# Weight units in a ring of six slots whose low part is written over the loaded data, in place of four raw slots and four split pairs

## The reference

```python
xn = rmsnorm(h, attn_norm[l])
proj = xn @ w_in[l]
y_mla = mla_branch(proj, q_norm[l], w_uq[l], kv_norm[l], w_ukv[l], cos, sin) @ w_mla_branch[l]
y_fox = fox_branch(proj, fox_f_bias[l]) @ w_fox_branch[l]
gates = jax.nn.sigmoid(proj[..., OFF_G:])
g_mla, g_fox = gates[..., :D_MODEL], gates[..., D_MODEL:]
h = h + (g_mla * y_mla + g_fox * y_fox) @ w_out[l]
hn = rmsnorm(h, mlp_norm[l])
u = jnp.square(jax.nn.relu(hn @ w_up[l]))
h = h + u @ w_down[l]
...
return rmsnorm(h, final_norm)
```

## Time and profile before

| | us |
|---|---|
| median of 3 runs | 1279.23 |
| lowest, highest | 1279.23, 1279.76 |
| profiled execution | 1279.13 |
| its span, first to last instruction | 1277.3 |
| TensorE matmuls busy | 1268.6 (99%) |
| weight loads of TensorE busy | 1053.9 (83%) |
| VectorE busy | 761.6 (60%) |
| ScalarE busy | 596.9 (47%) |
| GpSimd busy | 137.8 (11%) |

### The profile page before, as it was taken

How to read it: one execution, slowest core, us unless ns; L and a number is a source line. 1 busy time by engine, 2 the same in 40 slices (tenths; PEclk the granted TensorE clock), 3 DMA queues, 4 the chain that set the end, 5 groups by cost and what they waited for, 6 DMA issues and landing times.

```text
span 1277.3 us, 14314 instructions
## 1 busy us (share of the span) xinstructions
PE 1268.6 (99%) x5666; PEld 1053.9 (83%) x5666; DVE 761.6 (60%) x759; ACT 596.9 (47%) x688; POOL 137.8 (11%) x239
## 2 busy tenths in 40 slices
PE   9999999999999999999999999999999999999997
PEld 7888888888888888888888888888888888888886
DVE  6676566646766577566665655454455656554543
ACT  6654345444555444444454444333344444453443
POOL 0122001103221111110111110000000101100000
PEclk9999999999999999999999999999999999999999
DMA  8799856756887688787778786666667787856663
GB/s 329 250 295 277 260 176 214 230 188 200 272 266 213 203 297 276 233 249 228 253 229 259 224 260 194 195 196 195 189 222 235 235 246 237 285 168 215 195 197 116
DMA packets 82851, 293.88 MB, mean 230 GB/s; under 512 B 11288, under 2 KB 11872, under 8 KB 82144
## 3 DMA queue, kind: packets, MB, share of 16 engines
q1 hardware_dynamic: 67248, 243.04, 58.9%
q0 software_dynamic: 14528, 48.00, 13.1%
q10 hardware_dynamic: 1008, 1.92, 0.4%
HBM read 269.45 MB, written 23.47 MB: 229 GB/s over the span
## 4 chain that ended last, share of the span: by engine, by line
PE 99%; DVE 0%; ACT 0%; DVEq 0%; POOL 0%; issue 0%; ACTq 0%; POOLq 0%
PE bank L593 97%; PE bank L694 1%; PE bank L676 0%; PE bank L674 0%; PE bank L718 0%; PE bank L697 0%; PE bank L679 0%; PE bank L677 0%; DVE resid L1317 0%; DVE final L1326 0%; ACT square L983 0%; DVEq L335 0%; POOL kr_low L478 0%; ACT std_col L987 0%; DVE rstd_col L1323 0%
## 5 line engine op out<-in xcount | busy, mean ns | idle before, releaser
L1029 DVE TENSOR_TENSOR hl<-raw,hl 128x1024 fp32r<-128x1024 f32 x451 | 550.4, 1230 | 465.1 <-ACT hl L813 464.7
L813 ACT ACTIVATE hl<-raw 128x1024 fp32r<-128x1024 f32 x451 | 475.7, 1059 | 600.0 <-PE bank L593 570.5
L593 PE MATMUL bank<-hl,hn_hl 128*128 128x512 f32 x1536 | 348.5, 389 | 0.0
L593 PE MATMUL bank<-hl,u_hl 128*128 128x512 f32 x1536 | 348.5, 389 | 0.0
L593 PE MATMUL bank<-hl,x_hl 128*128 128x512 f32 (+1 forms) x1536 | 344.9, 385 | 0.0
L593 PEld LDWEIGHTS bank<-hl,hn_hl 128*128 128x128 f32 x1536 | 288.3, 188 | 59.9
L593 PEld LDWEIGHTS bank<-hl,u_hl 128*128 128x128 f32 x1536 | 288.3, 188 | 59.9
L593 PEld LDWEIGHTS bank<-hl,x_hl 128*128 128x128 f32 x1536 | 284.0, 188 | 56.8 <-DVE hl L1020 0.4
L593 PE MATMUL bank<-hl,m_hl 128*128 128x512 f32 x384 | 87.2, 389 | 0.0
L593 PEld LDWEIGHTS bank<-hl,m_hl 128*128 128x128 f32 x384 | 72.1, 188 | 15.0
L489 POOL DMA_DIRECT2D turn_rows<-blocks x35 | 19.7, 563 | 556.0 <-DVE blocks L1164 550.8
(11 more groups left out here) (149 smaller groups left out, 450.9 us busy)
## 6 DMA issues: line engine op xcount, KB each, us to landing
raw<-weights SPq DMA_DIRECT2D x454, 512.0 KB, 4.3
turn_rows<-blocks POOLq DMA_DIRECT2D x34, 512.0 KB, 3.6
turned<-turn_rows POOLq DMA_DIRECT2D x96, 128.0 KB, 5.3
prob_rows<-prob_blocks POOLq DMA_DIRECT2D x8, 384.0 KB, 2.8
prob_t<-prob_rows POOLq DMA_DIRECT2D x32, 96.0 KB, 5.3
turned_h<-turn_rows POOLq DMA_DIRECT2D x20, 128.0 KB, 5.3
x_rows<-x_n POOLq DMA_DIRECT2D x2, 1024.0 KB, 8.7
resid<-x_n POOLq DMA_DIRECT2D x1, 2048.0 KB, 9.4
```

The lines of the kernel that those rows point to most:

```text
L593: return nc.tensor.matmul(bank[:, gr.pair + tb, 0:gr.cols], tile[:, k, x_part, tb * P:tb * P + P], w, start=k == 0 and not x_part and not ...
L813: nc.scalar.activation(hl[:, slot, 0], raw[:, slot], ACT.Copy).then_inc(unit_hi, 1)
L1029: nc.vector.tensor_tensor(hl[:, slot, 1], raw[:, slot], hl[:, slot, 0].bitcast(F32), ALU.subtract).then_inc(unit_split, 1)
```

## The change

The two rings become three tiles with one slot number: `raw` and `low` lie at the same place (offset 0, six slots of 4 KB), `high` lies at 24 KB (six slots). Together they take the same 48 KB. ScalarE copies `raw` to `high`, VectorE subtracts `high` from `raw` and writes the result over `raw` under the name `low`, and TensorE reads `high` and `low`. A slot is therefore in use from its load to its last matmul, and the load of unit u waits for `unit_used` of unit u-6. ScalarE's wait for `unit_used` is gone: whoever has been loaded may be copied. SyncE's start now holds six units; the pieces of x are in the same places. LAG = 4 keeps what RING = 4 set otherwise: the distance in `make_due` and the four units of the last group.

```diff
-RING = 4
+
+RING = 6
+
+LAG = 4
...
-        due[min(unit + RING, N_UNITS - 1)].append((what, g))
+        due[min(unit + LAG, N_UNITS - 1)].append((what, g))
...
     raw = at("raw", 0, RING, UNIT)
-    hl = at("hl", 16 * kib, RING, 2, UNIT, dt=F32R)
+    low = at("low", 0, RING, UNIT, dt=F32R)
+    high = at("high", 24 * kib, RING, UNIT, dt=F32R)
...
-                c = x_columns(X_PIECES[n + 1])
-                sp.dma_start(x_in[:, c], x_t[:, c]).then_inc(x_loaded[n + 1], 16)
+                if n + 1 < len(X_PIECES):
+                    c = x_columns(X_PIECES[n + 1])
+                    sp.dma_start(x_in[:, c], x_t[:, c]).then_inc(x_loaded[n + 1], 16)
             for u in range(RING, N_UNITS):
-                sp.wait_ge(unit_split, u - RING + 1)
+                sp.wait_ge(unit_used, u - RING + 1)
                 sp.dma_start(raw[:, slot_of(u)], stream[u]).then_inc(unit_loaded[slot_of(u)], 16)
...
-                w = hl[:, slot_of(gr.unit[i]), w_part, gr.cols * s:gr.cols * s + gr.cols]
+                part = low if w_part else high
+                w = part[:, slot_of(gr.unit[i]), gr.cols * s:gr.cols * s + gr.cols]
...
-                ahead = gr.units - RING
+                ahead = gr.units - LAG
...
-                if u >= RING:
-                    act.wait_ge(unit_used, u - RING + 1)
...
-                nc.scalar.activation(hl[:, slot, 0], raw[:, slot], ACT.Copy).then_inc(unit_hi, 1)
+                nc.scalar.activation(high[:, slot], raw[:, slot], ACT.Copy).then_inc(unit_hi, 1)
...
-                nc.vector.tensor_tensor(hl[:, slot, 1], raw[:, slot], hl[:, slot, 0].bitcast(F32),
+                nc.vector.tensor_tensor(low[:, slot], raw[:, slot], high[:, slot].bitcast(F32),
                                         ALU.subtract).then_inc(unit_split, 1)
```

More of the change, by code:

```diff
@@ L805, in unit_to_hi @@
                         act.wait_ge(unit_loaded[slot], loaded)
-                    nc.scalar.activation(hl[:, slot, 0, 0:WIDE], raw[:, slot, 0:WIDE], ACT.Copy).then_inc(first_hi, 1)
+                    nc.scalar.activation(high[:, slot, 0:WIDE], raw[:, slot, 0:WIDE], ACT.Copy).then_inc(first_hi, 1)
                     if u == 0:
@@ L809, in unit_to_hi @@
                     act.wait_ge(unit_loaded[slot], loaded)
-                    nc.scalar.activation(hl[:, slot, 0, WIDE:], raw[:, slot, WIDE:], ACT.Copy).then_inc(unit_hi, 1)
+                    nc.scalar.activation(high[:, slot, WIDE:], raw[:, slot, WIDE:], ACT.Copy).then_inc(unit_hi, 1)
                     return
                 act.wait_ge(unit_loaded[slot], loaded)
-                nc.scalar.activation(hl[:, slot, 0], raw[:, slot], ACT.Copy).then_inc(unit_hi, 1)
+                nc.scalar.activation(high[:, slot], raw[:, slot], ACT.Copy).then_inc(unit_hi, 1)
             def root(norm, sums, d):
@@ L1019, in unit_to_lo @@
                     dve.wait_ge(first_hi, u + 1)
-                    nc.vector.tensor_tensor(hl[:, slot, 1, 0:WIDE], raw[:, slot, 0:WIDE],
-                                            hl[:, slot, 0, 0:WIDE].bitcast(F32), ALU.subtract).then_inc(first_split, 1)
+                    nc.vector.tensor_tensor(low[:, slot, 0:WIDE], raw[:, slot, 0:WIDE],
+                                            high[:, slot, 0:WIDE].bitcast(F32), ALU.subtract).then_inc(first_split, 1)
                     if u == 0:
@@ L1024, in unit_to_lo @@
                     dve.wait_ge(unit_hi, u + 1)
-                    nc.vector.tensor_tensor(hl[:, slot, 1, WIDE:], raw[:, slot, WIDE:],
-                                            hl[:, slot, 0, WIDE:].bitcast(F32), ALU.subtract).then_inc(unit_split, 1)
+                    nc.vector.tensor_tensor(low[:, slot, WIDE:], raw[:, slot, WIDE:],
+                                            high[:, slot, WIDE:].bitcast(F32), ALU.subtract).then_inc(unit_split, 1)
                     return
                 dve.wait_ge(unit_hi, u + 1)
-                nc.vector.tensor_tensor(hl[:, slot, 1], raw[:, slot], hl[:, slot, 0].bitcast(F32),
+                nc.vector.tensor_tensor(low[:, slot], raw[:, slot], high[:, slot].bitcast(F32),
                                         ALU.subtract).then_inc(unit_split, 1)
```

## The result

| us | before | after |
|---|---|---|
| median of 14 runs each, taken together | 1279.40 | 1281.28 |
| lowest, highest | 1278.98, 1280.79 | 1279.72, 1283.56 |
| profiled execution | 1279.13 | 1281.30 |
| its span | 1277.3 | 1279.5 |

The ratio is 1.0016, with a 95% interval of 1.0009 to 1.0023. The change costs 2 us. The median lies just above the end of the predicted range (1281.2) and 2.1 us above the forecast. The difference is smaller than the 0.2% that the prediction took for the least that can be told from no change, but the interval leaves 1.0000 out and the runs spread over 3.8 us where those of before spread over 1.8.

A forecast was written before the change was run, and what follows sets the result against it. TensorE's stream of matmuls without a hole was taken to bound the kernel. 1279.13 us + 0 for the stream + 0 for the ends = 1279.1, with the median's 0.1 1279.2; range 1278.4 to 1281.2.

The forecast's parts named there:

- TensorE bounds it at 227 ns a matmul: Whole kernel: TensorE takes matmuls without a hole, 226.7 ns each, 2.72 us per unit of two slabs.
- rival of the pace (2): Matmuls get longer or shorter with the rings 24 KB apart: 1284.7 or 1273.7 us; chance 0.03 longer, 0.02 shorter.
- A plain stretch: Ordinary units such as 200: split 6.8 us early at the median landing, 5.64 before; no TensorE stall, term 0.
- The latent norms: Near 60 us, unit 22, thinnest place: 0.8 us left before, 1.4 after, or a stall from 6.3 us landings; taken 0.
- Units 200 to 204: Place where ScalarE waits for VectorE: 2.5 us stay at 5.9 us landing, upper bound a 0.4 us stall; taken 0.
- the 16 places: Thin places: eight softmax steps, square chunks of w_out (four) and down1 (three), latent norms; each taken 0, at most 0.4 us.
- Units 12 and 13: Tightest units behind the start, their loads taking 8.6 and 8.9 us: 2 us left, term 0.
- rival 1: Late loads stall thin places from 8.0 us landings on; 0.4 us at all 16 gives 1285.6; chance in full 0.04.
- The start: Loads 4 and 5 leave earlier but stand longer in the same queue; gain at most 0.8 us, taken 0.
- The subtraction in place: VectorE's subtraction writes over its input, expected to stay at 1.23 us; a loss matters only from near a doubling.
- Rival 3: In-place subtraction much slower: at twice 1.23 us VectorE binds, about 1318 us; chance 0.01.
- the reading of the bound: Opening argument: time falls only if a matmul or the two ends get shorter, rises only if a unit is late.

The follow-up runs named there:

- after again: The changed kernel run again, unaltered: median 1281.51 us, ratio 1.0018 against the kernel before; its profiled execution took 1279.19.

## Why the prediction was right or wrong

**TensorE bounds it at 227 ns a matmul: right.** 226.7 ns over 3408 matmuls, and no rival of the pace (2) showed itself.

**A plain stretch, split ahead of need: right.** ScalarE waits for loads (571.3 us) and the load queue for TensorE (1093.8 us), as written; behind the start TensorE waits for no unit at all. Unit 200 is split 6.8 us ahead of its first matmul, the figure of the prediction.

**The latent norms: right.** 1.4 us left was the estimate. The three subtractions stand here:

```profile
61.29 3.96 DVE L1033 TENSOR_TENSOR low<-raw,high 128x1024 fp32r<-128x1024 f32 x3
```

Unit 22 is split at 61.29 + 3.96 / 3 = 62.6 and used at 64.1, 1.4 us left, where the prediction had 0.8 for before.

**Units 200 to 204: right, and on the safe side.** The argument was that bursts of loads go. In the first half of this stretch of after, loads issued from 560 to 575 us landed in

```profile
DMA to landing us min/median/max: 3.7/4.3/4.9
```

against 3.7/5.9/8.6 in the earlier trace rows; 4.9 us for unit 202 where 5.9 was taken, and unit 204 has 3.3 us left, where 2.5 were taken. The prediction worked one of the 16 places for all. Another, unit 196 in w_out, went from 2.5 us left to 1.3, and it is among those that stall where ScalarE's wait stays. Units 12 and 13 landed in 6.7 and 5.1 us instead of 8.6 and 8.9. From 20 us on the longest landing of all loads is

```profile
DMA to landing us min/median/max: 3.3/4.3/7.6
```

and rival 1, whose price began at 8.0, didn't come. In the profile of after again the longest is 8.4, and no unit was late there either.

**The start: right.** Loads 4 and 5 left at 5.8 and 6.3 and took 9.7 and 10.4 us; what left earlier stood in the same queue. TensorE's idle time at the first steps is 0.4 and 0.5 us, where the prediction had 0.4 and 0.4. Units 12 and 13 have 4.3 and 5.9 us left; their 2 us were too careful.

**The subtraction in place: right.** 1229 ns, against 1.23 us. Rival 3 has no ground.

**What failed** is the last step of the reading of the bound: "it rises only if a unit is late", and with it "what counts is how far ahead of its first matmul a unit is split". TensorE waits for two kinds of operand, and only the right one was looked at. The left one, `m_hl`, had 0.8 us left at 497.3, as thin as the thinnest unit, and it comes by DMA engines that the loads share. "Neither stalls TensorE. [...] the load is no longer held by VectorE. Term: 0" took the hold of the load queue for idle time only. It also kept the DMA engines clear while a turned chunk was written. In the profiled execution the missing term is 6.09 - 3.65 = 2.4 us on the write, 0.5 on what follows it, less 0.2 from an earlier issue: the chunk is ready at 499.3 instead of 496.6, and 2.7 - 0.8 = 1.9 us, with 0.1 for the hand-over, fall on TensorE. The prediction had the sign of this in its own facts: fewer bursts mean an even stream, and an even stream has no quiet stretch.

The rule from the Trainium skill (SBUF — State Buffer, "The DMA setup-cost knee") gave an estimate of 3.2 us for 512 KB. For the write it is near the trace only where little else is under way (2.9 us with the loads held, 3.6 in the median before); beside an even stream of loads the same write takes 5.4.

The range was too narrow by this one term. Its upper end was made of stalls of units, which didn't occur, and it came within 0.1 us of the median by chance. The other forecasts of this part, that no unit stalls and no pace changes, were right by their mechanism, and the time was wrong by a path that they left out.

## What to carry to other kernels

Before changing when a prefetch leaves, list every operand that the bound engine waits for, with what each has left, and not those of the changed ring alone; whatever comes by the same DMA engines is moved by the change as well. A wait that looks like idle time in a queue can be what keeps the engines clear for somebody else's urgent transfer. Where one transfer turns late, moving its consumer (one constant here) took the loss away, and holding other transfers back only moved the crowd.

## What was not expected of the hardware

- The same 512 KB write took 3.6 us in the median where loads paused (other transfers on the engines for 16% of its time) and 5.4 with one load of 512 KB every 2.72 us (56%), while the 128 KB reads behind it went from 5.3 to 4.6: the sum of both stages grew by only 1.1 us in the median.
- Three held loads that leave within 0.9 us, together with four reads of 128 KB, land in 3.6, 5.9 and 9.1 us.
- The kernel after spread over 6.1 us in its second set of runs (1279.10 to 1285.16) and over 0.85 us once one consumer stood 10.9 us later. A wide spread was here the sign of a place with nothing left.
